# High and low operand as one matmul of 512 columns in six of the products

## The reference

```python
x = x + g2 * ((relu(h @ w_up[i]) ** 2) @ w_down[i])   # i = 0, 1: "down0", "down1"
x = x + g1 * (o @ w_o)                                # "o", after the attention
y_a = silu(layernorm(u)) @ conv_w_out + conv_b_out    # "conv"
m = sigmoid(z_ga) * y_a + sigmoid(z_gb) * y_b
x = x + m @ w_mix_out                                 # "mix"
x = x + (silu(h @ ffn_w1) * (h @ ffn_w3)) @ ffn_w2    # "w2", then the final norm
```

## Time and profile before

| | |
|---|---|
| time, median of 3 runs | 1035.75 us (1035.46 to 1040.01) |
| the profiled execution's own time | 1040.98 us |
| its span, first to last instruction | 1039.2 us |
| mean granted PE clock | 0.987 |
| PE busy | 992.9 us (96%) |
| PEld busy | 938.6 us (90%) |
| DVE busy | 785.1 us (76%) |
| ACT busy | 524.6 us (50%) |
| mean share of the DMA engines, q1 | 59.4% |

### The profile page before, as it was taken

The page is one execution under the profiler, slowest core; times in us unless marked ns, Lnnn a source line. Parts: engine busy times, 40 slices in busy tenths (PEclk is TensorE's granted clock), DMA queues, the critical chain, the costliest instruction groups (busy, mean ns, idle before and its releaser), DMA issues.

```text
span 1039.2 us, 19948 instructions
## 1 busy us (share of the span) xinstructions
PE 992.9 (96%) x7918; PEld 938.6 (90%) x7918; DVE 785.1 (76%) x1443; ACT 524.6 (50%) x826; POOL 1.9 (0%) x14
## 2 busy tenths in 40 slices
PE   4699999999999989999999999999999999999996
PEld 1479999999989889999999989898889999999995
DVE  4769667888677688778666789898997787777554
ACT  3247754444665567665444535468116564444341
POOL 0000000000000000000000000000000000000000
PEclk8799999999999999999999999999999999999998
DMA  8998987787454765554555336363445455555531
GB/s 359 422 420 318 351 320 275 292 336 270 135 186 117 294 244 187 179 183 151 211 197 188 122 126 239 122 223 109 155 162 202 167 172 193 199 177 186 203 122 41
DMA packets 36327, 222.27 MB, mean 214 GB/s; under 512 B 4331, under 2 KB 9628, under 8 KB 9884
## 3 DMA queue, kind: packets, MB, share of 16 engines
q1 hardware_dynamic: 36252, 221.22, 59.4%
HBM read 220.13 MB, written 1.07 MB: 213 GB/s over the span
## 4 chain that ended last, share of the span: by engine, by line
PE 88%; DVE 4%; DMA 4%; ACT 2%; issue 1%; SPq 0%; DVEq 0%; ACTq 0%
PE bank L590 23%; PE bank L596 23%; PE bank L591 23%; PE bank L896 10%; DMA mod_raw<-w_mod 3%; PE bank L946 2%; PE s_banks L619 2%; DVE w_lo L1375 1%; PE s_banks L946 1%; DMA raw<-weights 1%; PE s_banks L590 1%; PE s_banks L591 1%; PE s_banks L596 1%; PE bank L648 1%; DMA x<-x_in 0%
## 5 line engine op out<-in xcount | busy, mean ns | idle before, releaser
L1375 DVE TENSOR_TENSOR w_lo<-raw,w_hi 128x1024 fp32r<-128x1024 f32 x268 | 325.0, 1218 | 28.1 <-ACT w_hi L1016 27.3
L1016 ACT ACTIVATE w_hi<-raw 128x1024 fp32r<-128x1024 f32 x268 | 280.4, 1052 | 115.0 <-PE bank L596 108.8
L590 PE MATMUL bank<-xg_hi,w_hi 128*128 128x258 f32 (+1 forms) x1248 | 310.5, 286 | 3.8 <-DVE x L1630 1.7
L591 PE MATMUL bank<-xg_lo,w_hi 128*128 128x258 f32 (+1 forms) x1248 | 305.4, 282 | 0.0
L590 PEld LDWEIGHTS bank<-xg_hi,w_hi 128*128 128x128 f32 x1248 | 235.6, 189 | 9.7 <-issue 5.4
L591 PEld LDWEIGHTS bank<-xg_lo,w_hi 128*128 128x128 f32 x1248 | 236.0, 189 | 0.2
L596 PE MATMUL bank<-xg_hi,w_lo 128*128 128x258 f32 (+1 forms) x1248 | 178.7, 282 | 0.0
L596 PEld LDWEIGHTS bank<-xg_hi,w_lo 128*128 128x128 f32 x1248 | 161.6, 189 | 0.0
L590 PE MATMUL bank<-hid_hi,w_hi 128*128 128x256 f32 x512 | 123.5, 280 | 1.5 <-DVE ab L1564 1.5
L591 PE MATMUL bank<-hid_lo,w_hi 128*128 128x256 f32 x512 | 123.5, 279 | 0.0
L1775 DVE SCALAR_TENSOR_TENSOR y<-u,vec,y 128x256 f32<-128x256 f32 x240 | 98.6, 483 | 0.2
(11 more groups left out here) (238 smaller groups left out, 1257.0 us busy)
## 6 DMA issues: line engine op xcount, KB each, us to landing
raw<-weights SPq DMA_DIRECT2D x157, 1024.0 KB, 5.0
mod_raw<-w_mod SPq DMA_DIRECT2D x32, 1024.0 KB, 11.7
mod_raw<-w_dots SPq DMA_DIRECT2D x16, 1024.0 KB, 8.2
toep<-bias_by_distance SPq DMA_DIRECT2D x8, 256.0 KB, 5.4
x<-x_in SPq DMA_DIRECT2D x1, 1024.0 KB, 5.1
toep<-bias_by_distance SPq DMA_DIRECT2D x8, 128.0 KB, 3.9
y_out<-yout SPq DMA_DIRECT2D x8, 128.0 KB, 1.8
c_all<-c_row SPq DMA_DIRECT2D x1, 512.0 KB, 7.3
```

Of the source, the lines that this page charges most:

```text
L590: pe.matmul(dst, hi, r_hi, start=start, stop=False, skip_group_check=True)
L591: pe.matmul(dst, hi, r_lo, start=False, stop=False, skip_group_check=True)
L1016: act.activation(pool_w_hi[:, at, :] if name == "pool" and at < 2 else w_hi[:, at % HL, :], raw[:, slot, (at % 2) * UT * P:(at % 2 + 1) * ...
L1375: ve.tensor_tensor(lo, raw[:, slot, (at % 2) * UT * P:(at % 2 + 1) * UT * P], hi.bitcast(F32), ALU.subtract).then_inc(lo_done, 1)
```

## The change

Each pair of operand tensors becomes one tensor with an axis of two: `hid`, `o`, `act`, `f` and `xg`, with `hid_hi` and so on as its halves. In down0, down1, w2, o, conv and mix, `by_high_wide` replaces the two matmuls of `by_high`: one matmul with `w_hi` as weights and 512 columns, 256 of the high and 256 of the low operand, into the two halves of the bank. `by_low` still adds into the first half. So a finished tile is the sum of the two halves, and somebody has to add them. In down0, down1, o, mix and w2 DVE does it with a second residual addition (`high_residual`, ahead of `residual`, which waits for its result, since both write `x`). In conv ACT copies the second half with the bias to `newt`, DVE adds the first half, and the product with the gate is an instruction of its own. The other phases keep their three matmuls of 256 or 258 columns. The diff shows the exchange on PE and the second addition for down; they stand in the same way in o, mix and w2 (and the exchange in conv).

```diff
+            def by_high_wide(bank, slot, s, both, start):
+                pe.matmul(bank.rearrange("p (a n) -> p a n", a=2), w_hi[:, slot, s * P:(s + 1) * P], both, start=start, stop=False,
+                          skip_group_check=True)
...
@@ down
-                    by_high(dst[:, 0:SEQ], (U0[name] + j) % HL, s, hid_hi[:, k, :], hid_lo[:, k, :], k == 0)
+                    by_high_wide(dst, (U0[name] + j) % HL, s, hid[:, :, k, :], k == 0)
...
@@ scalar engine, conv
             for m in range(8):
+                act.wait_ge(pe_units, U0["conv"] + m + 1)
+                act.activation(newt[:, m % 2, :], out_bank("conv", m)[:, SEQ:2 * SEQ], ACT.Identity, bias=col("cb", m))\
+                    .then_inc(high_copied, 1)
                 split("conv", 0, m)
                 act.wait_ge(m_done, m + 1)
                 act.activation(act_hi[:, m, :], sga[:, m, :], ACT.Copy).then_inc(act_hi_done, 1)
...
@@ vector engine
+            def high_residual(name, i, j, gate):
+                m = 2 * i + j
+                dst, src = chunk(x, m), (banks[j] if name == "w2" else out_bank(name, j))[:, SEQ:2 * SEQ]
+                if gate is None:
+                    ve.tensor_tensor(dst, src, dst, ALU.add).then_inc(high_read, 1)
+                else:
+                    g = modv[:, gate + m:gate + m + 1] if isinstance(m, int) else modv[:, bass.ds(m + gate, 1)]
+                    ve.scalar_tensor_tensor(dst, src, g, dst, ALU.mult, ALU.add).then_inc(high_read, 1)
...
@@ vector engine, down
                     ve.wait_ge(pe_units, 8 * i + (U0[name] + j + 1))
+                    high_residual(name, i, j // 4, gate)
+                    ve.wait_ge(high_read, 2 * i + (HIGH0[name] + j // 4 + 1))
                     residual(name, i, j // 4, gate)
...
@@ vector engine, conv
                 ve.wait_ge(pe_units, U0["conv"] + m + 1)
-                ve.scalar_tensor_tensor(sga[:, m, :], out_bank("conv", m)[:, 0:SEQ], col("cb", m), sga[:, m, :], ALU.add,
-                                        ALU.mult).then_inc(tile_read, 1)
+                ve.wait_ge(high_copied, m + 1)
+                ve.tensor_tensor(newt[:, m % 2, :], bank[:, 0:SEQ], newt[:, m % 2, :], ALU.add).then_inc(tile_read, 1)
                 if m:
                     split("conv", 0, m)
+                ve.wait_ge(tile_read, T0["conv"] + m + 1)
+                link(ve.tensor_tensor(sga[:, m, :], newt[:, m % 2, :], sga[:, m, :], ALU.mult))
                 if m:
                     low(RC + m - 1, m - 1, sga[:, m - 1, :], (m_done, m))
-                ve.wait_ge(tile_read, T0["conv"] + m + 1)
                 ve.tensor_tensor(sga[:, m, :], sga[:, m, :], sgb[:, m, :], ALU.add).then_inc(m_done, 1)
```

80 lines of the change are left out of this document (48 added, 32 removed).

## The result

The changed kernel takes 1052.45 us (median; 1051.53 to 1052.72), the kernel before, beside it, 1037.78 us (1035.46 to 1040.01): 1.0139 times as long, with a 95% interval of 1.0114 to 1.0163. That is 14.7 us slower, where the prediction had 1037.3 us and a range up to 1043.5. From one profiled execution to the other it is 1040.98 to 1052.72, only 11.74 us. The 3 us between the two differences turned out to be a part of the lesson: the profile that the prediction read was a slow draw of the kernel before.

A forecast was written before the change was run, and what follows sets the result against it. PE, busy for 96% of the span, was taken as the bound. Terms of -10.6 + 1.5 + 3.5 + 5.2 + 2.0 = +1.6 us gave 1042.6 against the profile, 1037.3 against the median; range 1030.5 to 1043.5.

The forecast's parts named there:

- price of the wide matmul: down0, down1, w2: 0.218 us replaces a pair of 0.2358 or 0.2266, saving 9.1 and 1.5, together 10.6 us.
- conv: conv: a turn becomes a circle through ACT and DVE of 3.55 us; mix's last chunk starts 5.0 us late.
- mix: mix: only the second addition at the end is lost (+0.46); ffn's last chunk 5.2 us late, conv included.
- the clock: Pause ahead of mix's last chunks: one fall of the clock, costing 1 to 2.5 us, taken as 2.
- o: o: DVE's turn grows to 2.78 us, longer than PE's unit; the last xg_lo for up1 comes 3.5 us later.
- The step to the median: Whole kernel: 1042.6 us against the profiled execution becomes 1037.3 against the median 1035.75, 5 us lower by run to run.
- Rival B: Wide matmuls: half the saving, with the excess paid once for each instruction; chance 0.22.
- Rival C: Wide matmuls: no saving, with an excess that belongs to the columns; chance 0.08.
- One more read at each end: Ends of down0, down1 and w2: the second addition adds 0.52, 0.52 and 0.46, together 1.5 us.
- slower: Whole kernel: a time over 1040.9 us; chance 0.27.

The follow-up runs named there:

- bench: Kernel without the computation, timing rows of matmuls alone, DVE and ACT first idle, then busy: fp32r with 512 columns 226.7 to 233.1 ns, bf16 215.8.
- one_read: The whole change, but the second half of the bank is not added in o and w2, leaving out that part of the product: 1047.31 us.
- fill: The whole change, with useless matmuls of 512 columns in PE's three pauses ahead of mix's chunks 5, 6 and 7: 1052.13 us.
- conv_ahead: The whole change, but ACT copies the second half of conv's next tile before making act_hi of the current one: 1045.43 us, 1.0066 times before.
- bench3: Kernel without the computation, PE alone: units of 24 fp32r matmuls behind one fp32r matmul of 0 to 192 columns; 113.3 or 117.9 ns with 256 columns.
- bench4: Kernel without the computation, PE alone, at the kernel's addresses: all 68 units behind a short fp32r matmul at 117.8 ns, the four without one at 113.3.

## Why the prediction was wrong, point by point

The forecast missed the measured median by 15.2 us. From the terms, profile against profile: 7.1 are the price of the wide matmul, 1.7 conv, mix and the clock, 0.3 o, 1.1 the later start of down0. The other 4.9 are the step from the profile to the median.

- **The price of the wide matmul is the step that failed most.** No run shows the 0.218 us that was taken; the wide matmul measures 0.229. A bf16 matmul of the same 512 columns takes 215.8 ns and fp32r 226.7 at the least: type, not length, sets the excess. down gave 3.4 us net of its reads, not 8.1, and w2 lost 0.9 on PE where it was to win 1.5. In sum these are 4.7 and 2.4 us. Rival B, given 0.22, had half the saving, with the excess paid once for each instruction; by bench fp32r's is 6.7 ns at 256 columns and 13.5 at 512. Rival C, given 0.08, had no saving, with an excess that belongs to the columns: the right cause for most of it, though in down a pair of 235.8 became 229. The native row is no measure of the price: its (4.26 - 0.38) / 18 = 0.2155 is one of two records of a matmul (the 144 native matmuls of glu and rg are 288 records, and in bench a record takes 215.9 ns), so a native matmul takes 0.431 and is no instance of 512 columns in one instruction.
- **The step to the median.** The sum said +1.6 against the profiled 1040.98, and the prediction then took off 5.2 us "by run to run". The changed kernel's profile and median differ by 0.3. A part of the 5.2 was a low draw of three runs: later sets of 7 to 19 runs of before have medians of 1037.65 to 1038.73, not 1035.75. The rest, 2.3 to 3.3 us, fits a profile that had both down stages in the slow rhythm, by bad luck: no other of the four traces of before has. The changed kernel has no such draw to make. Its down stages take 89.56 to 89.63 us in all fourteen cases of its trace and six of its variants'. So those 5 us did not hit both kernels alike, and could not be subtracted. The rhythm of the unprofiled runs is not known.
- **One more read at each end**: 0.52 as worked out at down0; at the end 0.46, as the pause ahead of the last sum goes from 1.70 to 2.16.
- **o**: 3.5 forecast, 3.75 measured, by the mechanism named: without the second read o gets back 3.1 us (one_read). PE's pause ahead of up1, from start to start, was 2.07 us and not 4, since PE lost time itself at half clock; without that fall it was 3.4 and 3.6 (fill, conv_ahead).
- **conv**: circle 3.55 forecast, 3.60 measured; the last chunk at 826.3 forecast, 828.34 found, of which 1.43 is conv's later start. Right in mechanism and size.
- **mix**: ffn's last chunk starts at 854.8 in place of 844.53, less the 1.43 again 8.9 us late. 5.2 were forecast for it, 2.5 are the clock, and part of the rest is again the price: mix's wide matmuls take 0.235 in the median, a unit 2.77 us and not 2.65, and with conv undone mix and ffn are still 0.85 us longer than before.
- **The clock**: a fall in the new pause was right, its length wrong (10.2 us, where 6.8 was taken from the early fall to 0.50), its cost of 2.0 measures 2.5. The fall in o, which was not foreseen there, cost nothing.
- Conv, mix, ffn and the clock together: 7.2 forecast, 8.9 measured. The chance of 0.27 for slower was too small: with no saving on PE the forecast's own other terms already gave 1035.75 + 12.2 = 1047.9. That the change costs time through the circle in conv was forecast; that its saving would vanish was not.

## What to carry to other kernels

Time a matmul in its own type before a saving is built on merging two of them: here fp32r takes 226.7 to 233 ns for 512 columns, and a row of another type (bf16 215.8, a native record 215.9) says nothing on it. Where an engine's copy is written behind its wait for the other engine, two instructions of half a microsecond become a circle: the turn of both engines grows to 3.6 us where PE's unit takes 2.8. Moving the copy one step ahead gave back 7 of 14.7 us. And when a profile and the median of runs differ, find the stage in which they do before the difference is subtracted: a change can take away the lucky case and nothing else.

## What was not expected of the hardware

- Rows of fp32r matmuls with 256 columns have two stable rhythms on the same data, 113.3 and 117.8 ns, held for 90 us. Both occur in the kernel, with DVE, ACT and transfers at work, and in bench3, with all of them idle. A short matmul ahead can change which one, differently for other addresses: behind 192 columns all units settle at 113.3 in bench3 and run at 117.8 in bench4, at the kernel's addresses. The cause is not known.
- fp32r takes 226.7 to 233 ns for 512 columns, bf16 215.8. A native float32 matmul of 256 columns stands as two records of 215.9 ns each, 0.43 us in all.
- In the changed kernel the granted clock fell to 0.50 in o behind pauses of 1.0 and 1.6 us, three microseconds apart (window at 369.4); in conv_ahead and fill it stayed full there, behind the same pauses, and fell at 387 us, where up1 begins (0.57 and 0.58 over 387 to 391).
